# Prompt sparse attention: the compressed branch's 16 keys padded to 128

## What is computed

```
lc = einsum(q, kc) * scale + bias        # compressed keys: one per 16 tokens, 15 for the prompt
pc = masked_softmax(lc);  o_c = pc @ vc
o_s = softmax(q ks + bias) @ vs          # selected blocks (all 256 prompt tokens here)
o_w = softmax(q kw + bias) @ vw          # window of 512 tokens
o_n = g0 * o_c + g1 * o_s + g2 * o_w     # gates
```

## Time and profile before

| what | us |
|---|---|
| median of three runs (2202.96 to 2205.05) | 2203.04 |
| the profiled execution's own time | 2206.43 |
| its span | 2204.3 |
| PE busy in the span | 1879.3 (85%) |
| DVE busy | 1042.0 (47%) |
| ACT busy | 536.3 (24%) |
| POOL busy | 92.3 (4%) |

### The profile page before, as it was taken

The page is one execution under the profiler, slowest core; times in us unless marked ns, Lnnn a source line. Parts: engine busy times, 40 slices in busy tenths (PEclk is TensorE's granted clock), DMA queues, the critical chain, the costliest instruction groups (busy, mean ns, idle before and its releaser), DMA issues.

```text
span 2204.3 us, 29369 instructions
## 1 busy us (share of the span) xinstructions
PE 1879.3 (85%) x11296; PEld 1602.7 (73%) x11296; DVE 1042.0 (47%) x1538; ACT 536.3 (24%) x770; POOL 92.3 (4%) x119
## 2 busy tenths in 40 slices
PE   6999899945766797766889999799998976799998
PEld 5999867735556574333679998599997753699995
DVE  5666400546421543444166663266652372566632
ACT  3333200121101332111033332143321131333320
POOL 0000000022022110100000000000000000000000
PEclk9999999955567555666899999899999987899999
DMA  4444333194042282233234442334433254244431
GB/s 177 146 143 173 117 127 120 67 323 161 1 137 82 61 274 71 68 96 103 65 140 142 146 174 73 120 117 150 172 133 118 103 219 191 77 149 142 164 117 62
DMA packets 64069, 287.67 MB, mean 131 GB/s; under 512 B 10276, under 2 KB 31808, under 8 KB 40160
## 3 DMA queue, kind: packets, MB, share of 16 engines
q1 hardware_dynamic: 58832, 266.98, 34.5%
q0 software_dynamic: 5168, 19.76, 3.0%
HBM read 280.51 MB, written 41.62 MB: 146 GB/s over the span
## 4 chain that ended last, share of the span: by engine, by line
PE 73%; issue 11%; DVE 9%; ACT 2%; DMA 2%; POOL 1%; POOLq 1%; SPq 1%; DVEq 0%; ACTq 0%
PE ps L589 13%; PE ps L591 13%; PE ps L590 13%; PE ps L600 11%; PE ps L1211 3%; PE ps L1911 2%; PE ps L1458 1%; DVE w_lo L580 1%; PE ps L1123 1%; PE ps L1334 1%; ACT w_hi L574 1%; PE ps L519 1%; PE ps L1443 1%; DVE live L532 1%; PE ps L1474 1%
## 5 line engine op out<-in xcount | busy, mean ns | idle before, releaser
L589 PE MATMUL ps<-x_hi,w_hi 128*128 128x320 f32 x1408 | 440.1, 313 | 41.6 <-DVE x_lo L541 37.4
L590 PE MATMUL ps<-x_lo,w_hi 128*128 128x320 f32 x1408 | 438.9, 312 | 0.0
L591 PE MATMUL ps<-x_hi,w_lo 128*128 128x320 f32 x1408 | 438.7, 312 | 0.0
L580 DVE TENSOR_TENSOR w_lo<-live,w_hi 128x2048 fp32r<-128x2048 f32 (+1 forms) x120 | 300.7, 2506 | 186.7 <-ACT w_hi L574 186.7
L574 ACT ACTIVATE w_hi<-mem 128x2048 fp32r<-128x2048 f32 (+1 forms) x120 | 250.5, 2088 | 263.1 <-DVE mem L568 263.1
L589 PEld LDWEIGHTS ps<-x_hi,w_hi 128*128 128x128 f32 x1408 | 268.0, 190 | 44.6 <-issue 39.3
L590 PEld LDWEIGHTS ps<-x_lo,w_hi 128*128 128x128 f32 x1408 | 268.0, 190 | 0.0
L591 PEld LDWEIGHTS ps<-x_hi,w_lo 128*128 128x128 f32 x1408 | 267.7, 190 | 0.0
L600 PE MATMUL ps<-live 128*128 128x320 f32 x832 | 234.6, 445 | 20.8 <-DVE live L532 13.9
L568 DVE TENSOR_SCALAR mem<-live 128x2048 int32<-128x2048 int32 (+1 forms) x120 | 159.9, 1333 | 155.5 <-PE ps L591 141.9
L600 PEld LDWEIGHTS ps<-live 128*128 128x128 f32 x832 | 162.8, 196 | 91.7 <-issue 28.2
(11 more groups left out here) (364 smaller groups left out, 2126.3 us busy)
## 6 DMA issues: line engine op xcount, KB each, us to landing
live<-in_w_fi SPq DMA_DIRECT2D x88, 1024.0 KB, 4.8
live<-in_w_fo SPq DMA_DIRECT2D x32, 1408.0 KB, 6.0
mem<-in_dil SPq DMA_DIRECT2D x16, 1152.0 KB, 11.1
out_old_dil<-in_old_dil SPq DMA_DIRECT2D x8, 2032.0 KB, 29.3
live<-in_w_even SPq DMA_DIRECT2D x12, 1024.0 KB, 4.8
live<-in_w_gate SPq DMA_DIRECT2D x8, 1024.0 KB, 4.8
out_old_dil<-in_old_dil SPq DMA_DIRECT2D x8, 1008.0 KB, 35.9
live<-in_cmp POOLq DMA_DIRECT2D x32, 192.0 KB, 3.9
```

The lines of the kernel that those rows point to most:

```text
L580: nc.vector.tensor_tensor(w_lo[:, slot, 0:w], ring[:, slot, 0:w], w_hi[:, slot, 0:w].bitcast(F32), ALU.subtract).then_inc(w_split.sem, 1)
L589: nc.tensor.matmul(out, wh, hi, start=first_k, stop=False)
L590: nc.tensor.matmul(out, wh, lo, start=False, stop=False)
L591: return nc.tensor.matmul(out, wl, hi, start=False, stop=last_k)
```

## The change

The compressed branch of the prompt gets its own value tile of 128 rows, 16 filled and 112 zero, and its weights in `pl` get 128 columns, 112 of them zero for good. Its transpose is 128x128, its copy out of PSUM has 128 partitions, and its output matmul has 128 rows. Vector writes the zeros: 128x192 in the compression stage, with a wait of its own engine behind it, ahead of the copy of the 16 rows; and 128x3x112 ahead of the first turn. No copy, load or semaphore is added beside these. `pl` grows by 336 elements a partition and moves `ppt` and `pst`; the value tiles together stay as large as before.

```diff
-        vc = sb([64, NB + 1, NKV * HD])
+        vc = sb([64, NB, NKV * HD])
+        vc_prompt = sb([P, NKV * HD])
...
-        pl = sb([P, 3, 528])
+        pl = sb([P, 3, 640])
...
-            nc.vector.tensor_copy(vc[0:16, NB, :], ps[0:16, 7, 0:192]).then_inc(cm_vc.sem, 1)
+            chain(nc.vector.memset(vc_prompt[:], 0.0))
+            chain.settle()
+            nc.vector.tensor_copy(vc_prompt[0:16, :], ps[0:16, 7, 0:192]).then_inc(cm_vc.sem, 1)
...
-                nc.tensor.matmul(ps[r, 6 + s, 0:P], vc[0:16, NB, HD * kv:HD * kv + HD], ppt[0:16, s, 512:640],
+                nc.tensor.matmul(ps[r, 6 + s, 0:P], vc_prompt[:, HD * kv:HD * kv + HD], ppt[:, s, 512:640],
                                  start=False, stop=True).then_inc(pa_o.sem, 1)
...
-                nc.tensor.transpose(ps[0:16, 6 + s, P:2 * P], pl[:, t % 3, 512:528], ident[:]).then_inc(pa_tr.sem, 1)
+                nc.tensor.transpose(ps[:, 6 + s, P:2 * P], pl[:, t % 3, 512:640], ident[:]).then_inc(pa_tr.sem, 1)
...
-                nc.vector.tensor_copy(ppt[0:16, t % 2, 512:640], ps[0:16, 6 + t % 2, P:2 * P]).then_inc(pa_ptc.sem, 1)
+                nc.vector.tensor_copy(ppt[:, t % 2, 512:640], ps[:, 6 + t % 2, P:2 * P]).then_inc(pa_ptc.sem, 1)
+            chain(nc.vector.memset(pl[:, :, 528:640], 0.0))
             logits(0)
```

## The result

The changed kernel takes 2165.35 us (median of 4 runs, 2161.52 to 2168.17), the kernel before beside it 2203.07 (2202.96 to 2205.05): a ratio of 0.9826 with a 95% interval of 0.9809 to 0.9843, or 37.7 us less. On another occasion it took 2165.92 against 2204.15 (0.9821, 0.9803 to 0.9839). The forecast was 2167.5, from 2160 to 2190. The profiled execution took 2168.17 us with a span of 2166.0 at a mean granted clock of 0.883; before it was 2206.43, 2204.3 and 0.859.

The account below looks back on a forecast made before the run. TensorE, always busy at 1.2 GHz, was taken to bound the prompt stage. Pairs at 2.4 GHz gain 35.2 us, earlier pairs 0.9, zeros cost 0.6: 2203.0 - 35.5 = 2167.5 us, range 2160 to 2190.

Parts of the forecast that it names:

- The pause: TensorE, ahead of the 16-row output: a new run costs 0.19 us a turn, 4.6 us in all; padding removes it.
- The transposes: TensorE, prompt turns: padding the transpose saves nothing; its longer weight load stays hidden, or costs 1.9 us in all.
- The zeros and the copy: Vector: two memsets ahead of the turns cost 0.6 us; the copy of turned weights stays at 0.27 us.
- The clock: TensorE, prompt stage: rises from 1.2 to 2.4 GHz after some 20 us, as in the odd layer's loop; chance 0.72.
- rivals 1, 2 and 4: Clock stays at 1.2 GHz: 2199.0 us, 0.13; rises and falls back: about 2185, 0.10; padding joins no runs: 2203.6, 0.02.
- rival 3: Prompt turns: the pause only moves behind the padded output, and longer loads and copies cost time; 2212 us, chance 0.03.
- The pair: Two prompt turns at 2.4 GHz: a loop through four engines takes 6.2 us in place of 9.90, gaining 3.7.
- The number of pairs: Prompt turns: 9.5 of 12 pairs run at 2.4 GHz, gaining 35.2 us; the 2.5 before gain 0.9.
- Not lost behind the stage: After the prompt stage: the gain of 35.5 us stays, as only the remainder of the cache-row copy competes.

Follow-up runs that it names:

- the first four experiments: Against the changed kernel: 16-row output, 2202.64 us; unpadded transpose, 2166.66; 64-row output, 2172.12. Against the kernel before: compressed output left out, 2171.96.

## Why the prediction was right

**The pause.** Forecast: 0.19 us a turn ahead of the 16-row output, gone with 128 rows. Measured: the six at 1.47 us, no idle time of the weight load. Right.

**The transposes.** Forecast: nothing saved, nothing paid. Right: alone they change nothing, and the longer load stays hidden.

**The zeros and the copy.** Forecast: 0.6 us for the memsets, no change of the copy. Measured: 0.25 + 0.26 = 0.5 us, and 284 ns a copy against 272, 12 ns more for the other 112 partitions. Right.

**The clock.** Forecast, by likeness with the odd layer's loop: a rise to 2.4 GHz that stays. It rose, and stayed at 1.00 with TensorE busy for 8.19 of 10 us, so rivals 1, 2 and 4 fall; rival 3 falls with the pause, which went. The reason given, that the 16-row instructions and their pause set the two loops apart, stands for the two together: with them the clock stays (2202.64 us), without them, padded or left out, it rises. The runs by size, where the row of 16 is the run with the padded transposes alone:

| rows of the compressed output | four outputs and it, at 1.2 GHz, us | clock rises, us after the first scores | median, us |
|---|---|---|---|
| 16 | 1.66 | not in the stage | 2202.64 |
| 32 | 1.66 | not in the stage | 2204.5 |
| 64 | 1.66 | 38.8 | 2172.12 |
| 80 | 1.48 | 18.3 | 2165.37 |
| 128 | 1.47 | 18.3 | 2165.35 |
| left out | | 52.8 | 2171.96 |

From 32 to 64 rows, with the pause in place, the rise comes; from 64 to 80, with the pause gone, it comes sooner. Which quantity the chip looks at is not shown by this, nor which share is the pause's and which the rows'.

One reading of the odd loop was wrong. The 3.6 us without a gap that the prediction gives it before its rise only count from 1800, where the earlier trace rows begin; TensorE's last idle time there ended at 1796.17, so it was 1803.6 - 1796.17 = 7.4 us. That line, and the last gap at the beginning of the even prompt's turns, in the changed kernel and in the kernel before:

```profile
1796.17 0.90 PE L2024 MATMUL ps<-live,mem 128*128 128x128 f32 x3 [2.71 <-DVE mem L2086]
```

```profile
741.35 0.69 PE L1477 MATMUL ps<-live,mem 128*128 128x128 f32 x2 [1.54 <-POOL mem L1519]
```

```profile
741.51 0.69 PE L1474 MATMUL ps<-live,mem 128*128 128x128 f32 x2 [1.54 <-POOL mem L1516]
```

In the changed kernel TensorE ran for 751.6 - 741.35 = 10.3 us without a gap before the clock rose, with 64 rows for 30.7; in the kernel before it ran so from 741.51 to 846.5, 105 us, and the clock never rose. So work without a gap did not by itself bring the clock up here; the loops differ in their instructions.

The rule of the Trainium skill (TensorE: Matmul & The Clock Gate, Part 4: PE-mode transpose), that transposes don't count as work for the clock gate in the way that other matmuls do, led to 1.2 GHz throughout. The trace disagrees with that outcome: the clock rose, also where the transposes were left as they were (at 750.6 us with the output alone padded). Whether transposes count in part no run here shows.

**The pair.** Forecast 6.2 us, 6.14 measured, and term by term in the chain above: logits and scaling up to GpSimd 786.15 - 783.67 = 2.48 (forecast 1.49 + 0.99), GpSimd and hand-over 0.66 (0.70), the rest from 786.81 to 789.81 3.00 (0.47 + 1.23 + 1.1 + 0.2). That the loop is the bound is shown by the edits that shorten it: outputs out of it, GpSimd out of it, the pair falls to 5.7 and 5.64. One estimate beside the sum was too low: TensorE's own work doesn't halve from 9.5 to 4.8 us a pair, it takes 5.2. Every pair measured is that work and one wait: 5.2 + 0.91, 0.49, 0.41, 0.69 and, with the copy early, 0.30 us. So a new order of the same work can't bring a pair below 5.2, and the last one is 0.30 from it.

**The number of pairs** is the term that was mis-sized. Forecast: 9.5 of 12 at 2.4 GHz, 35.2 us. The 39.5 us won in the turns are at 9.90 - 6.14 = 3.76 a pair worth 10.5. The clock rose 18.3 us after the first scores, in place of some 20, but that is the smaller part: the first outputs come only 12.4 us after the first scores (745.68 - 733.32), so by the rise the outputs of about one pair had run and not of two and a half.

**Not lost behind the stage**: right in the main. The projection that follows gained 41.2 - 39.95 = 1.2 us more at the higher clock, and the sample stage took 2.5 longer. TensorE waited 27.1 us in five waits for the loads of selected cache rows there, against 26.1, which is 1.0 of the 2.5. It is not a price of the earlier start: with the padded transposes alone the stage began at 859.5 us, nearly as late as before, and took 178.9 us as well, and with 64 rows it began at 827.0 and took 176.6. Over all the runs it took 176.4 to 179.0, with a cause that stays open.

The turns gave some 4 us more than forecast and what lies behind them some 2 less. That the forecast came within 2.2 us of the median is therefore in part luck.

## What to carry to other kernels

A stage whose engine is never idle can still run at half of its clock (10.00 of 10 us at 0.50 here): read the granted clock beside the busy share, and compare the stage with one of the same kind that does get 2.4 GHz. Instructions with few rows in the middle of full ones can cost more than their own time: two of them took 0.61 us here, in place of 0.42. Padding them with zeros was nearly free, and it was enough to make them tall enough to join the run beside them. When the clock doubled, the bound moved to the loop through the other engines. There the place of a step in the order counted like its work, and gains did not add up: GpSimd's scaling on Vector took 5.2 us out of the stage, the outputs first 3.6, both together 1.9, and the outputs first with one 0.28 us copy moved 4.2.

## What was unexpected

The pause is there with 16, 32 and 64 rows and gone with 80, with the whole of its 0.19 us; beyond that, more rows bring no earlier rise and no shorter time.

The rise is repeatable where it comes early. In all nine traces with 80 or 128 rows, whatever the order and the filler, it came 18.2 to 18.4 us after the first scores, though these started up to 3 us apart.

With few rows it seems to come by chance. Of the 13 runs of the kernel before beside the first four experiments four took 2192.11 to 2196.02 us at mean clocks of 0.864 to 0.870, against 0.861 to 0.863 of the other nine; of 13 on another occasion two took 2189.74 and 2191.68 at 0.869 and 0.870. With the padded transposes alone one of ten took 2185.96 at 0.876. That the clock rose late in this stage there is inferred from the mean and not shown by a trace.
